# A trunk layer with differential attention on eight cores: first loads packed piece by piece, and an earlier gate for the first V pieces

## The chip, the cores and the metric

The kernel runs on the 8 cores of one Trainium2 chip. Every core runs the same program on its own part of the sequence. The metric is the device time of the slowest core in microseconds, and the time shown is the median of the runs.

## What is computed

The reference is one layer of a decoder trunk on x (4 batches, 4096 positions, 1024 channels, float32). Cut to what matters:

```python
z = h @ w_in                    # (B, S, 3072): q, k, v, attention gate, pool input, pool gate, 512 columns each
o = diff_attention(q, k, v, lam)            # causal, 4 heads, two softmaxes per head, their difference times v
attn_out = rms_norm(o, subln_g) * (1 - lam_init) * silu(g_attn)
pool_out = multiscale_pool(u, w_pool, scale) * silu(g_pool)     # trailing means over 2, 4, 8, 16 positions
h = layer_norm(ALPHA * h + concat(attn_out, pool_out) @ w_out)
h = h + (p @ w_pe) * sigmoid(h @ w_pg + b_pg)
```

## The kernel before

A batch belongs to two cores. Its 4096 positions are four groups of eight blocks of 128 positions; of each group a core owns four blocks and computes their output, and for the other four it computes only K and V, which its own queries need. The projections, the attention, the pooling and the output stage of a core are one long program on TensorE, in which the attention of a group (QK, exp on ScalarE, PV) is woven into the projections of the next one.

**What sets the order.** Every step is a node with a cost, the buffers that it reads and writes, and a key. The planner (class Sched, its run at L264) simulates the engines and the DMA rings: on each engine it takes the node with the smallest key among those that are ready. The instructions are then written out in that order, each with the semaphore waits that its buffers need (Prog.op, Prog.dma, Prog.flush). A gate on a load is a buffer in its list of reads: the issuing engine waits for what last wrote that buffer. Issues of DMAs have the key -10000, so they go first on their engine. All DMA instructions of the trace are put down to L153, the line in flush that issues them, and all matmuls of the kernel's helper mmf to L542.

**The start.** Two weights and two blocks of x are wanted first. They come in five pieces along the contraction index k (eight chunks of 128): PIECES = (0,2), (2,4), (4,6), (6,7), (7,8). A chunk is 128 rows of 512 float32, so a piece of two chunks is 128 rows of 4 KB, a piece of one is 128 rows of 2 KB.

- SP loads the five pieces of the own blocks' x (xT_d[1]) and ACT the five pieces of the K weight (win_d[SEC_K]) as float32 into a staging area that is later mixT. Neither waits for anything.
- For each piece DVE casts x to bf16 (L607) into X[:, 0] and ACT casts K's weight (L609) into its place in W (win).
- POOL loads the five pieces of the V weight (win_d[SEC_V]) straight into W, cast to bf16 on the way. The list GI says for which x piece each V piece waits: GATES[i] is the staging buffer of x piece GI[i], counted from 0.
- Behind them POOL loads the five pieces of the other blocks' x (xT_d[0]) into X[:, 1], then the whole weight sections Q, a block of constants (cst), GA, a halo (xh), U, GP and w_pool. All of these wait for the last x piece (GATE).

TensorE runs twelve matmuls on zeros as a warm-up and then three projections whose loop over the pieces is outermost (function outer, L1151): K of the own blocks (v1, with five warm-up matmuls behind each of the first three pieces), V of the own blocks (v2) and K of the other blocks (v3), 32 matmuls each. Piece i of a projection waits for piece i of the weight and of x. Their keys are fixed numbers counted up in hk, so their order on TensorE is fixed. Behind v3 come V of the other blocks, Q, and the rest by the planner.

In the trace sb_mixT<-xT are SP's x pieces, sb_mixT<-w_in ACT's K pieces, sb_W<-w_in POOL's V pieces and sections, and sb_X<-xT POOL's pieces of the other x, and later whole blocks of x (load_x, L592). The matmuls of v1 and v3 are psum_all<-sb_X,sb_W, those of v2 psum_all<-sb_W,sb_X, and V of the other blocks again psum_all<-sb_W,sb_X.

Before the change the host lays x out as [8 groups of blocks][128 partitions][8 chunks][512] and w_in as [6 sections][128 partitions][8 chunks][512], so the rows of a piece are 16 KB apart.

Of the kernel before, what the change touches and what calls it, by code (L numbers as in the profile page):

```python
# [20 lines left out]
POOL_W = (2, 4, 8, 16)  # L21
OWN = {0: [0, 3, 4, 7], 1: [1, 2, 5, 6]}
VW = 130
GI = (3, 4, 4, 4, 4)
PIECES = [(0, 2), (2, 4), (4, 6), (6, 7), (7, 8)]
SEC_Q, SEC_K, SEC_V, SEC_GA, SEC_U, SEC_GP = range(6)

# [42 lines left out]
class Prog:  # L70
# [48 lines left out]
    def dma(self, Q, out, in_, ds, reads=(), writes=(), turn=False):  # L119
        self._deps(Q, reads, writes)  # L120
        ds.cnt += 16
        t = (ds.sem, ds.cnt)
        _SNAP[(ds.sem.num, ds.cnt)] = dict(Q.seen)
        Q.ops.append(("turn" if turn else "dma", out, in_, ds.sem))
        self._mark(t, reads, writes)
# [327 lines left out]
def build_nc():  # L453
# [3 lines left out]
    xT_d = din("xT", [8, 128, 8, GT])  # L457
# [3 lines left out]
    win_d = din("w_in", [6, 128, 8, 512])  # L461
# [10 lines left out]
    with ExitStack() as top:  # L472
        P = Prog(nc, top)
        PE, ACT, DVE, POOL, SP = P.PE, P.ACT, P.DVE, P.POOL, P.SP

        def sb(name, shape, dt):
            return top.enter_context(nc.sbuf_tensor("sb_" + name, shape, dt))
# [9 lines left out]
        X = sb("X", [128, 2, 8, GT], BF16)  # L487
# [28 lines left out]
        win = W[:].rearrange("p (s k n) -> p s k n", s=6, k=8)  # L516
# [4 lines left out]
        B_x = [[Buf() for _ in PIECES] for _ in range(2)]  # L521
        B_st = [[Buf() for _ in PIECES] for _ in range(2)]
        B_w = [[Buf() for _ in (PIECES if s in (SEC_K, SEC_V) else [0])] for s in range(6)]
# [58 lines left out]
        def dma(Q, out, in_, reads, writes, kb, key=None, ds=None, run=4096):  # L582
            G.add([(Q, 650.0 if Q is POOL else 430.0 if Q is ACT else 400.0, None)], reads, writes, dma=(out, in_, ds or P.dsem(), kb, False, run),
                  key=key, slack=-1e4)
# [11 lines left out]
        def load_sec(s):  # L596
            dma(POOL, win[:, s], win_d[s], GATE, B_w[s], 2048)

        GATE, GATES = [B_st[0][4]], [[B_st[0][k]] for k in GI]
        stage = mixT[:].rearrange("p a n -> p (a n)").bitcast(F32).rearrange("p (s k n) -> p s k n", s=2, k=8)  # L600
        for i, (a, z) in enumerate(PIECES):
            s = slice(a, z)
            dma(SP, stage[:, 0, s, :], xT_d[1][:, s, :], [], [B_st[0][i]], 256 * (z - a))
            dma(ACT, stage[:, 1, s, :], win_d[SEC_K][:, s, :], [], [B_st[1][i]], 256 * (z - a))
        for i, (a, z) in enumerate(PIECES):
            s = slice(a, z)
            G.add([(DVE, 75 + (z - a) * 278.0, [lambda e, s=s: e.tensor_copy(out=X[:, 0, s, :], in_=stage[:, 0, s, :])])],  # L607
# [1 line left out]
            G.add([(ACT, CA((z - a) * 512), [lambda e, s=s: e.activation(out=win[:, SEC_K, s, :], in_=stage[:, 1, s, :], func=AF.Copy)])],  # L609
                  [B_st[1][i]] + B_mix[4 + a // 2], [B_w[SEC_K][i]])  # L610
        for i, (a, z) in enumerate(PIECES):
            dma(POOL, win[:, SEC_V, a:z, :], win_d[SEC_V][:, a:z, :], GATES[i], [B_w[SEC_V][i]], 256 * (z - a))
        for i, (a, z) in enumerate(PIECES):
            dma(POOL, X[:, 1, a:z, :], xT_d[0][:, a:z, :], GATE, [B_x[1][i]], 256 * (z - a))
        load_sec(SEC_Q)
        dma(POOL, cst, cst_d, GATE, [B_cst] + B_U, 546)
        load_sec(SEC_GA)
# [636 lines left out]

_NC_CACHE = {}

def _host_inputs(x, p, w_in, lam_q1, lam_k1, lam_q2, lam_k2, subln_g, w_pool, pool_scale,
                 w_out, ln_g, ln_b, w_pe, w_pg, b_pg):
    f = lambda a: np.ascontiguousarray(np.asarray(a, dtype=np.float32))
    x, p = f(x), f(p)  # L1260
    rows = lambda a, k: np.ascontiguousarray(f(a).reshape(k, 128, -1).transpose(1, 0, 2))
    common = {
        "w_in": np.ascontiguousarray(f(w_in)[0].reshape(8, 128, 6, 512).transpose(2, 1, 0, 3)),
        "w_pool": np.ascontiguousarray(f(w_pool)[0].transpose(1, 0, 2)),
        "w_out": rows(f(w_out)[0], 8), "w_pe": rows(f(w_pe)[0], 2), "w_pg": rows(f(w_pg)[0], 8),
        "ln_g": f(ln_g)[0].reshape(1, 1024), "ln_b": f(ln_b)[0].reshape(1, 1024), "b_pg": f(b_pg)[0].reshape(1, 1024),
    }
    lamv = np.concatenate([f(lam_q1)[0], f(lam_k1)[0], f(lam_q2)[0], f(lam_k2)[0]])
    rep = lambda v: np.broadcast_to(v, (128, v.size))
    pscale = f(pool_scale)[0].reshape(4, 128).T  # L1270
    kk = np.arange(128)[:, None]
    qq = np.arange(128)[None, :]
    tri = (qq >= kk).astype(np.float32)
    in_maps = []
    for c in range(8):
        b, r = c // 2, c % 2
        own, oth = OWN[r], OWN[1 - r]
        xb = x[b].reshape(4, 8, 128, D_MODEL)
        xT = np.empty((8, 128, 8, GT), np.float32)
        for g in range(4):  # L1280
            for k, blks in ((0, oth), (1, own)):
                xT[2 * g + k] = xb[g][blks].reshape(GT, 8, 128).transpose(2, 1, 0)
        x_own = np.ascontiguousarray(xb[:, own].reshape(2048, D_MODEL))
        xh = np.zeros((4, 4, 16, D_MODEL), np.float32)
        for g in range(4):
            for i, o in enumerate(own):
                s = (8 * g + o) * 128
                if s > 0:
                    xh[g, i] = x[b, s - 16:s]
        xh = np.ascontiguousarray(xh.reshape(4, 64, 8, 128).transpose(0, 3, 2, 1))  # L1290
        pT = np.ascontiguousarray(p[0, b].reshape(4, 8, 128, 256)[:, own].reshape(2048, 2, 128).transpose(2, 1, 0))
        masks = np.zeros((128, 2, 2, 128), np.float32)
        for par in range(2):
            masks[:, par, 1, :] = tri
            masks[:, par, 0, :] = 1.0 if (par == 1) == (r == 0) else 0.0
        cnt = np.zeros((128, 4, 16), np.float32)
        t = np.arange(16, dtype=np.float32)
        for pi, w in enumerate(POOL_W):
            cnt[:, pi, :] = 1.0 / np.minimum(t + 1.0, float(w)) if own[0] == 0 else 1.0 / float(w)
        m = dict(common)  # L1300
        cst = np.ascontiguousarray(np.concatenate([rep(f(subln_g)[0]), pscale, cnt.reshape(128, 64), rep(lamv),
                                                   np.eye(128, dtype=np.float32), masks.reshape(128, 512)], axis=1))
        m.update({"xT": xT, "x_own": x_own, "xh": xh, "pT": pT, "cst": cst})
        in_maps.append(m)
    return in_maps
# [13 lines left out]
```

How the kernel before makes its waits and increments, by code:

```python
        def run(S, e):  # L135
            pend = []
            for o in S.ops:
                if o[0] == "wait":
                    pend.append(o)
                elif o[0] == "op":
                    for w in pend[:-1]:
                        e.wait_ge(w[1], w[2])
                    ins = o[1](e)
                    if pend:
                        ins._wait_ge(pend[-1][1], pend[-1][2])
                    pend = []
                    if o[2]:
                        ins.then_inc(S.sem, 1)
                else:
                    for w in pend:
                        e.wait_ge(w[1], w[2])
                    pend = []
                    (e.dma_start_transpose if o[0] == "turn" else e.dma_start)(out=o[1], in_=o[2]).then_inc(o[3], 16)
            for w in pend:
                e.wait_ge(w[1], w[2])
            S.ops = []
```

## Time and profile before

| | us |
|---|---|
| median of 3 runs | 598.72 (598.18 to 599.36) |
| the profiled execution | 599.14 |
| its span on the slowest core, core 3 | 597.6 |
| spans of its eight cores | 592.3 to 597.6 |
| TensorE busy on core 3 | 581.3 (97%) |
| ScalarE, VectorE, GpSimd busy on core 3 | 370.5, 347.8, 81.9 |
| DMA on core 3 | 40311 packets, 48.84 MB, mean 82 GB/s |

Times of rows count from the first instruction of the core's span. Engines are PE (TensorE, with PEld for its weight loads), DVE (VectorE), ACT (ScalarE), POOL (GpSimd) and SP (SyncE). GB/s and the size of a DMA count the bytes written, so a load that casts float32 to bf16 reads twice what is shown. PEclk is the granted clock of TensorE as a share of full speed.

### The profile page before, as it was taken

The page shows a single profiled execution, that of the slowest core. Times are in us where ns is not written, and L with a number is a line of the kernel's source. Part 1 is how long each engine was busy: PE and PEld are TensorE (multiplying, and loading weights), DVE is VectorE, ACT ScalarE, POOL GpSimd, SP SyncE. Part 2 cuts the span into 40 slices and gives each one's busy share as a digit, 9 for nine tenths or more (in the row PEclk, how much of TensorE's full clock was granted, in tenths as well). Part 3 has the DMA queues.
Part 4 walks back from the last instruction along what each step waited for, and adds up shares of the span by engine and source line. Part 5 has one row for each costly group of instructions (what it writes and reads, how often), then busy time and mean ns, then how long its engine had stood idle before and what let it go on. Part 6 is the DMA issues. An engine that isn't in the chain of part 4 may idle for free.

```text
span 597.6 us, 12491 instructions; the slowest of 8 cores (592.3 to 597.6 us)
## 1 busy us (share of the span) xinstructions
PE 581.3 (97%) x5265; PEld 327.3 (55%) x5265; DVE 347.8 (58%) x839; ACT 370.5 (62%) x504; POOL 81.9 (14%) x110
## 2 busy tenths in 40 slices
PE   6889999999999999999999999999999999999996
PEld 2334544454555555666666565676665566565443
DVE  1111892149344386343434578877666787778887
ACT  1213634454654565878788887887887686766342
POOL 0601300040000300000022012021100010010210
PEclk8989999999999999999999999999999999999999
DMA  7799733100340004020654037222413443334442
GB/s 226 128 176 174 135 63 58 36 10 15 70 78 1 9 16 78 6 74 8 126 100 80 2 59 185 36 69 83 129 22 92 100 93 100 82 95 109 110 129 106
DMA packets 40311, 48.84 MB, mean 82 GB/s; under 512 B 30016, under 2 KB 31424, under 8 KB 38592
## 3 DMA queue, kind: packets, MB, share of 16 engines
q0 software_dynamic: 8672, 19.57, 19.8%
q1 hardware_dynamic: 30864, 26.39, 16.0%
q10 hardware_dynamic: 720, 2.10, 1.2%
q8 instruction: 41, 0.67, 0.5%
q14 instruction: 14, 0.11, 0.1%
HBM read 52.73 MB, written 8.39 MB: 102 GB/s over the span
## 4 chain that ended last, share of the span: by engine, by line
PE 87%; DMA 5%; DVE 4%; issue 1%; POOL 1%; ACT 1%; SPq 0%; DVEq 0%; POOLq 0%; ACTq 0%
PE psum_all L542 65%; PE psum_all L830 22%; DMA sb_mixT<-xT 3%; DMA sb_X<-xT 2%; DVE sb_X L570 1%; DVE sb_X L562 1%; DVE sb_W L570 1%; POOL sb_W L153 0%; DVE sb_st L984 0%; ACT sb_W L992 0%; ACT sb_PT L805 0%; POOL sb_mv L1000 0%; DVE sb_gps L570 0%; POOL sb_ms L860 0%; SPq L153 0%
## 5 line engine op out<-in xcount | busy, mean ns | idle before, releaser
L805 ACT ACTIVATE sb_PT<-psum_all 128x1024 bf16<-128x1024 f32 (+1 forms) x276 | 263.7, 1009 | 65.3 <-PE psum_all L542 65.1
L542 PE MATMUL psum_all<-sb_X,sb_W 128*128 128x512 bf16 x640 | 153.8, 384 | 5.7 <-ACT sb_W L609 3.7
L830 PE MATMUL psum_all<-sb_Vt,sb_PT 128*128 128x129 bf16 x2176 | 156.3, 220 | 0.0
L830 PEld LDWEIGHTS psum_all<-sb_Vt,sb_PT 128*128 128x128 bf16 x2176 | 132.2, 98 | 41.7 <-issue 12.8
L542 PEld LDWEIGHTS psum_all<-sb_X,sb_W 128*128 128x128 bf16 x640 | 59.8, 99 | 73.1 <-issue 6.7
L542 PE MATMUL psum_all<-sb_W,sb_X 128*128 128x512 bf16 x384 | 92.2, 380 | 2.0 <-DMA sb_W<-w_in 2.0
L542 PE MATMUL psum_all<-sb_mixT,sb_kT 64*128 64x128 bf16 (+2 forms) x1288 | 83.7, 255 | 0.0
L542 PE MATMUL psum_all<-sb_W 128*128 128x512 bf16 (+1 forms) x328 | 79.7, 374 | 0.5 <-DVE sb_W L580 0.5
L562 DVE TENSOR_TENSOR sb_PT<-sb_PT,sb_masks 128x256 bf16<-128x256 bf16 x128 | 39.8, 319 | 66.9 <-ACT sb_PT L805 65.9
L542 PEld LDWEIGHTS psum_all<-sb_mixT,sb_kT 64*128 64x128 bf16 x1288 | 42.8, 94 | 46.2 <-ACT sb_PT L805 20.3
L542 PE MATMUL psum_all<-sb_W,sb_mixT 128*128 128x512 bf16 x256 | 62.3, 379 | 0.3 <-ACT sb_PT L805 0.3
L542 PEld LDWEIGHTS psum_all<-sb_W,sb_X 128*128 128x128 bf16 x384 | 34.9, 98 | 40.2 <-DMA sb_W<-w_in 3.4
L570 DVE SCALAR_TENSOR_TENSOR sb_X<-sb_X,sb_mv,sb_MI 128x1024 f32<-128x1024 f32 (+1 forms) x33 | 41.2, 1247 | 7.6 <-POOL sb_mv L1000 7.4
L860 POOL TENSOR_TENSOR sb_ms<-sb_ms,sb_mhalf 128x3 f32<-128x3 f32 (+1 forms) x24 | 22.7, 945 | 165.1 <-DVE sb_ms L570 165.0
L542 PEld LDWEIGHTS psum_all<-sb_W 128*128 128x128 bf16 x328 | 29.6, 98 | 27.7 <-issue 1.4
L570 DVE SCALAR_TENSOR_TENSOR sb_gps<-sb_gps,psum_all 128x512 f32<-128x512 f32 (+1 forms) x49 | 32.9, 672 | 16.1 <-ACT sb_gps L552 14.5
L542 PEld LDWEIGHTS psum_all<-sb_W,sb_mixT 128*128 128x128 bf16 x256 | 23.3, 98 | 23.5 <-ACT sb_PT L805 0.5
L552 ACT ACTIVATE sb_gps<-psum_all 128x512 f32<-128x512 f32 (+1 forms) x37 | 21.7, 585 | 21.6 <-PE psum_all L542 21.3
L570 DVE SCALAR_TENSOR_TENSOR sb_X<-sb_X,psum_all 128x512 f32<-128x512 f32 x32 | 21.9, 684 | 18.8 <-PE psum_all L542 18.7
L579 ACT ACTIVATE sb_kT<-psum_all 128x512 bf16<-128x512 f32 x24 | 14.1, 597 | 28.3 <-PE psum_all L542 28.1
L562 DVE TENSOR_TENSOR sb_MI<-sb_MI 128x572 f32<-128x572 f32 (+3 forms) x40 | 29.5, 737 | 0.7
L570 DVE SCALAR_TENSOR_TENSOR sb_mixh<-sb_TA,sb_ms,sb_ga 128x128 bf16<-128x128 f32 x64 | 22.3, 349 | 12.9 <-POOL sb_ms L860 11.9
(98 smaller groups left out, 375.7 us busy)
## 6 DMA issues: line engine op xcount, KB each, us to landing
sb_X<-x_own SPq DMA_DIRECT2D x16, 512.0 KB, 3.7
sb_X<-xT POOLq DMA_DIRECT2D x6, 1024.0 KB, 8.4
out<-sb_X SPq DMA_DIRECT2D x12, 512.0 KB, 3.3
sb_W<-w_in POOLq DMA_DIRECT2D x4, 1024.0 KB, 31.4
sb_W<-w_out POOLq DMA_DIRECT2D x1, 2048.0 KB, 15.3
sb_W<-w_pg POOLq DMA_DIRECT2D x2, 1024.0 KB, 8.6
out<-sb_X SPq DMA_DIRECT2D x7, 256.0 KB, 2.1
sb_mixT<-w_in ACTq DMA_DIRECT2D x3, 512.0 KB, 13.3
```

Of the source, the lines that this page charges most:

```text
L542: return lambda e: e.matmul(out(), lhsT, rhs, start=start, stop=stop, skip_group_check=skip)
L552: G.add([(ACT, CA(n), [lambda e: e.activation(out=out, in_=in_(), func=func, scale=scale)])], reads, writes, slack=slack)
L562: fn = lambda e: e.tensor_tensor(out=out, in0=a() if callable(a) else a, in1=b, op=op)
L570: dve(lambda e: e.scalar_tensor_tensor(out=out, in0=c(a), scalar=s, in1=c(b), op0=op0, op1=op1), reads, writes, n, slack)
L579: G.add([(ACT, CA(n), [lambda e: e.activation(out=out, in_=in_(), func=AF.Copy)]), (DVE, CD(n * x), [lambda e: e.tensor_copy(out=out, in_= ...
L805: G.add([(ACT, CA(2 * w), [lambda e, vb=vb, w=w, pb=pb: e.activation(out=PT[:, pb, :, 0:w], in_=ps[:, vb[0].real:vb[0].real + 2, 0:w], fun ...
L830: return e.matmul(ps[:, 6 + c, col:col + 129], PT[:, pb, c, o:o + 128], Vt[:, kb, h, 0:129], start=st, stop=False, skip_group_check=True)
L860: G.add([(POOL, 350.0 + 210 * np_, [lambda e: e.tensor_tensor(out=ms[:, 1, 0:np_], in0=ms[:, 1, 0:np_], in1=mhalf[:, 0:np_], op=ALU.pow)]) ...
```

## The change

GI goes from (3, 4, 4, 4, 4) to (2, 3, 4, 4, 4): V piece 0 waits for x piece 2, V piece 1 for x piece 3, the others for x piece 4 as before. The host writes the pieces of the K weight, the V weight and of the first two blocks of x (own and other) one behind the other, each piece as [128][its chunks][512], and the loads read them there through the new helper part. The tiles on the chip, the casts and the matmuls stay as they are.

```diff
--- before.py
+++ after.py
@@ -21,7 +21,7 @@
 POOL_W = (2, 4, 8, 16)
 OWN = {0: [0, 3, 4, 7], 1: [1, 2, 5, 6]}
 VW = 130
-GI = (3, 4, 4, 4, 4)
+GI = (2, 3, 4, 4, 4)
 PIECES = [(0, 2), (2, 4), (4, 6), (6, 7), (7, 8)]
 SEC_Q, SEC_K, SEC_V, SEC_GA, SEC_U, SEC_GP = range(6)
 
@@ -596,12 +596,16 @@
         def load_sec(s):
             dma(POOL, win[:, s], win_d[s], GATE, B_w[s], 2048)
 
+        def part(src, a, z):
+
+            return src.rearrange("p k n -> (p k n)")[a * 65536:z * 65536].rearrange("(p k n) -> p k n", p=128, k=z - a)
+
         GATE, GATES = [B_st[0][4]], [[B_st[0][k]] for k in GI]
         stage = mixT[:].rearrange("p a n -> p (a n)").bitcast(F32).rearrange("p (s k n) -> p s k n", s=2, k=8)
         for i, (a, z) in enumerate(PIECES):
             s = slice(a, z)
-            dma(SP, stage[:, 0, s, :], xT_d[1][:, s, :], [], [B_st[0][i]], 256 * (z - a))
-            dma(ACT, stage[:, 1, s, :], win_d[SEC_K][:, s, :], [], [B_st[1][i]], 256 * (z - a))
+            dma(SP, stage[:, 0, s, :], part(xT_d[1], a, z), [], [B_st[0][i]], 256 * (z - a))
+            dma(ACT, stage[:, 1, s, :], part(win_d[SEC_K], a, z), [], [B_st[1][i]], 256 * (z - a))
         for i, (a, z) in enumerate(PIECES):
             s = slice(a, z)
             G.add([(DVE, 75 + (z - a) * 278.0, [lambda e, s=s: e.tensor_copy(out=X[:, 0, s, :], in_=stage[:, 0, s, :])])],
@@ -609,9 +613,9 @@
             G.add([(ACT, CA((z - a) * 512), [lambda e, s=s: e.activation(out=win[:, SEC_K, s, :], in_=stage[:, 1, s, :], func=AF.Copy)])],
                   [B_st[1][i]] + B_mix[4 + a // 2], [B_w[SEC_K][i]])
         for i, (a, z) in enumerate(PIECES):
-            dma(POOL, win[:, SEC_V, a:z, :], win_d[SEC_V][:, a:z, :], GATES[i], [B_w[SEC_V][i]], 256 * (z - a))
+            dma(POOL, win[:, SEC_V, a:z, :], part(win_d[SEC_V], a, z), GATES[i], [B_w[SEC_V][i]], 256 * (z - a))
         for i, (a, z) in enumerate(PIECES):
-            dma(POOL, X[:, 1, a:z, :], xT_d[0][:, a:z, :], GATE, [B_x[1][i]], 256 * (z - a))
+            dma(POOL, X[:, 1, a:z, :], part(xT_d[0], a, z), GATE, [B_x[1][i]], 256 * (z - a))
         load_sec(SEC_Q)
         dma(POOL, cst, cst_d, GATE, [B_cst] + B_U, 546)
         load_sec(SEC_GA)
@@ -1254,6 +1258,10 @@
 
 _NC_CACHE = {}
 
+def _in_pieces(a):
+
+    return np.concatenate([a[:, s:e].ravel() for s, e in PIECES]).reshape(a.shape)
+
 def _host_inputs(x, p, w_in, lam_q1, lam_k1, lam_q2, lam_k2, subln_g, w_pool, pool_scale,
                  w_out, ln_g, ln_b, w_pe, w_pg, b_pg):
     f = lambda a: np.ascontiguousarray(np.asarray(a, dtype=np.float32))
@@ -1265,6 +1273,8 @@
         "w_out": rows(f(w_out)[0], 8), "w_pe": rows(f(w_pe)[0], 2), "w_pg": rows(f(w_pg)[0], 8),
         "ln_g": f(ln_g)[0].reshape(1, 1024), "ln_b": f(ln_b)[0].reshape(1, 1024), "b_pg": f(b_pg)[0].reshape(1, 1024),
     }
+    for k in (SEC_K, SEC_V):
+        common["w_in"][k] = _in_pieces(common["w_in"][k])
     lamv = np.concatenate([f(lam_q1)[0], f(lam_k1)[0], f(lam_q2)[0], f(lam_k2)[0]])
     rep = lambda v: np.broadcast_to(v, (128, v.size))
     pscale = f(pool_scale)[0].reshape(4, 128).T
@@ -1280,6 +1290,8 @@
         for g in range(4):
             for k, blks in ((0, oth), (1, own)):
                 xT[2 * g + k] = xb[g][blks].reshape(GT, 8, 128).transpose(2, 1, 0)
+        for k in range(2):
+            xT[k] = _in_pieces(xT[k])
         x_own = np.ascontiguousarray(xb[:, own].reshape(2048, D_MODEL))
         xh = np.zeros((4, 4, 16, D_MODEL), np.float32)
         for g in range(4):
```

## Rows read from the trace of the kernel before

**Rows 1.** Spans of the cores, with the mean granted clock.

```profile
core 3: 597.6 us, clock 0.993
...
core 5: 597.4 us, clock 0.990
...
core 7: 592.3 us, clock 0.997
```

**Rows 2.** Engines by stretch, core 3: length, busy time (instructions), clock, DMA share, GB/s.

```profile
44.00:144.00 100.00, 100.00 (x637) 49.13 (x636) 50.35 (x130) 45.66 (x81) 17.04 (x20) 1.00 0.42 74
```

**Rows 3.** All waits of PE from 44 us to the end: in total, times, longest.

```profile
PE psum_all L1044 <- DVE sb_W L570: 0.8, 1, 0.8
PE psum_all L542 <- DVE sb_W L580: 0.5, 1, 0.5
PE psum_all L872 <- DVE sb_mv L574: 0.5, 1, 0.5
PE psum_all L542 <- ACT sb_PT L805: 0.3, 1, 0.3
```

**Rows 4.** Chain that ended last, core 3, 0 to 46 us: start, length, what.

```profile
2.44 15.89 DMA sb_mixT<-xT
...
19.68 0.52 issue
20.20 2.09 POOL sb_W L153 x4
22.29 12.14 DMA sb_X<-xT
```

**Rows 5.** Timeline of core 3: start, length, instruction, idle time before it and releaser.

```profile
17.01 0.69 DVE L607 CAST sb_X<-sb_mixT 128x1024 bf16<-128x1024 f32 x1 [2.65 <-DMA sb_mixT<-xT]
...
18.36 0.43 DVE L607 CAST sb_X<-sb_mixT 128x512 bf16<-128x512 f32 x1 [0.66 <-DMA sb_mixT<-xT]
...
19.66 0.43 DVE L607 CAST sb_X<-sb_mixT 128x512 bf16<-128x512 f32 x1 [0.88 <-DMA sb_mixT<-xT]
...
24.50 1.90 PE L542 MATMUL psum_all<-sb_W,sb_X 128*128 128x512 bf16 x8 [1.03 <-DMA sb_W<-w_in]
...
34.88 8.75 PE L542 MATMUL psum_all<-sb_X,sb_W 128*128 128x512 bf16 x32 [2.01 <-DMA sb_X<-xT]
...
43.47 6.85 PE L542 MATMUL psum_all<-sb_W,sb_X 128*128 128x512 bf16 x31
```

**Rows 6.** Timeline of core 7: second K projection and what follows it.

```profile
31.52 7.07 PE L542 MATMUL psum_all<-sb_X,sb_W 128*128 128x512 bf16 x32 [0.30 <-issue]
...
38.42 7.07 PE L542 MATMUL psum_all<-sb_W,sb_X 128*128 128x512 bf16 x32
```

**Rows 7.** Stretches of the start on core 3, columns as in rows 2.

```profile
2.40:8.00 5.60, 5.21 (x12) 1.55 (x12) 0.00 (x0) 1.28 (x1) 0.00 (x0) 1.00 0.89 208
8.00:13.00 5.00, 2.21 (x8) 0.97 (x9) 0.69 (x1) 1.06 (x1) 0.00 (x0) 0.87 0.99 302
2.40:18.30 15.90, 12.19 (x36) 4.22 (x37) 2.08 (x3) 4.44 (x4) 0.00 (x0) 0.89 0.88 261
18.30:19.70 1.40, 1.40 (x8) 0.64 (x7) 0.46 (x2) 0.64 (x2) 0.70 (x1) 1.00 0.06 22
19.70:21.00 1.30, 1.30 (x8) 0.59 (x7) 0.39 (x1) 0.63 (x1) 0.80 (x2) 1.00 0.18 5
21.00:34.40 13.40, 9.90 (x44) 3.80 (x42) 2.58 (x4) 2.17 (x4) 7.66 (x15) 1.00 1.00 124
34.40:39.50 5.10, 4.62 (x14) 1.83 (x15) 0.00 (x0) 0.00 (x0) 0.00 (x0) 0.67 1.12 193
```

**Rows 8.** DMA of core 3 from 44 to 66 us.

```profile
DMA packets 809, 3.93 MB, mean 179 GB/s; under 512 B 91, under 2 KB 335, under 8 KB 391
```

**Rows 9.** DMA of core 3 from 569 to 573 us, GB/s in 40 slices of 0.1 us.

```profile
GB/s 0 0 0 0 0 0 0 0 0 0 0 164 164 164 0 0 0 0 246 164 369 246 614 287 369 614 246 451 532 246 369 0 0 0 0 0 0 0 0 0
DMA packets 144, 0.52 MB, mean 131 GB/s; under 512 B 16, under 2 KB 16, under 8 KB 144
```

## The prediction

> **What bounds the kernel now.** I read the cores first. The time is that of the slowest core, core 3, with core 5 next and core 7 the fastest, 5.3 us less than core 3 [rows 1]. The question is where core 3 loses these 5.3 us, and the answer lies before 44 us. From 44 to 144 us its TensorE is busy for all of 100.00 us [rows 2], and from 44 us to the end the waits that TensorE has on other engines are four, 0.8, 0.5, 0.5 and 0.3 us, 2.1 us together [rows 3]. So whatever time the start gives up or wins is carried to the end nearly one for one. The two cores show it: the next work behind the second K projection begins at 43.47 us on core 3 and at 38.42 us on core 7 [rows 5, 6], 5.05 us apart, and the spans differ by 5.3.
>
> The start is bound by transfers. The chain of core 3 [rows 4] reads: 15.89 us until the fourth x piece has landed, behind it (not shown) POOL's issue of the first V piece, a pause of 0.52 us until POOL has the fifth piece, 2.09 us for the four other V issues, and 12.14 us from the issue of the other block's first x piece to its landing, which lets TensorE go on. The timeline of the same stretch [rows 5] shows TensorE's side of it: it stands still for 1.03 us before the first V piece and for 2.01 us before the second K projection, which waits for x. That projection then takes 8.75 us for 32 matmuls, 7.07 on core 7 [rows 6]: the granted clock of 34.4 to 39.5 us was 0.67 [rows 7], a mean of the two levels 1.2 and 2.4 GHz, right behind the waiting. The stretches of the DMA [rows 7] show two kinds of limit. From 2.4 to 18.3 us and from 21.0 to 34.4 us the engines are busy, shares 0.88 and 1.00: there their rate counts. Between the two, from 18.3 to 21.0 us, they move almost nothing (shares 0.06 and 0.18): the first loads are done and the V pieces, which POOL may issue only once x pieces four and five are in, have not begun.
>
> **The change part by part.** *The gate.* V piece one now waits for x piece three instead of four, V piece two for four instead of five, the other three for five as before. On core 3 these pieces are in, by the start of their casts [rows 5], at 17.01, 18.36 and 19.66 us. So the first V issue moves by 18.36 - 17.01 = 1.35 us, the second by 19.66 - 18.36 = 1.30. Nothing stands in POOL's queue ahead of them, and behind the fifth gate there are three V issues in place of four; at 2.09 / 4 = 0.52 us each [rows 4], the x issues and the weight sections behind them come 0.52 us earlier. What that does to the landing of x has two ends. If only its own issue counted, it would be 0.52 us. If the engines are what it waits for, it is the whole 1.35 us, because the V bytes then begin earlier in a stretch where the engines had nothing to do. The share of 1.00 from 21.0 us on speaks for the second, and I take 1.35. Do the earlier V bytes get in the way of the last x and K pieces? V data begins to move some 2.5 us behind its gate (gate at 18.36, a rate of 5 GB/s in 19.7 to 21.0 and full load only after, rows 5 and 7). From a gate at 17.01 that is about 19.5 us, and the first loads have only 22 GB/s left from 18.3 to 19.7. On core 3 the two hardly meet: nothing. On a core whose pieces come further apart they would meet, but what the last K pieces lose there the V pieces have won, and the second K projection waits for both.
>
> *The layout.* The same bytes go in transfers of the same number and size, from the same queues; on the chip's side a row of a piece stays one run of 4 KB (2 KB for the two small pieces), and rows now follow each other without the 16 KB step. No row shows this for these loads, so I bound it. The chain holds 15.89 + 12.14 = 28.0 us of transfer. The rate now is 261 GB/s in the first loads and, because the V and x pieces are cast on the way and the page counts the written half, 2 x 124 = 248 GB/s read in 21.0 to 34.4 us [rows 7]. The lower end is a stretch of the same rows: from 2.4 to 8.0 us the first loads ran at 208 GB/s. The upper end are the whole weight sections, which lie in one piece in memory with rows of 16 KB: 179 GB/s written from 44 to 66 us, that is up to 358 read [rows 8]. The nearest row by far is an x_own load, 128 rows of 4 KB that follow each other in memory, just what the pieces become: 0.52 MB between 570.1 and 572.1 us [rows 9], 260 GB/s, though alone on the engines. That is the rate of today. I stay close to it and take a tenth of the way to the upper end, (358 - 261) / 10, some 10 GB/s or 4%: 28.0 x (1 - 261 / 271) = 1.03 us.
>
> Here a rule speaks against the layout as a gain. The Trainium skill, DMA: Bandwidth & Descriptors, section "Latency and other measured facts", has copies at a row pitch of 512 KiB near full rate (207 of 214 GB/s) and a clear loss only from a pitch of 2 MiB up. By that rule a pitch of 16 KB costs nothing, the second term is zero and the sum is 1.35 us; the x_own row agrees, with 260 beside 261 GB/s.
>
> *The order.* The planner puts the gates into its own clock, so it may write another order. Up to the second K projection TensorE's order hangs on fixed keys. Behind it the V, x and weight transfers all move together. What a new order could win is at most the 2.1 us of waits left [rows 3]; what it could lose I bound by as much again, and I take zero, since the same work meets the same transfers a little earlier.
>
> *The sum.* 1.35 + 1.03 = 2.4 us off the profiled execution, which took 599.14 us (its span of 597.6 and 1.5 around it): 596.7. The median of the runs shown is 598.72, 0.42 below the profiled one, so the same step gives 596.3. All of that holds if core 3 stays typical of the slowest core; core 5, 0.2 us behind it, has the same gates.
>
> **The rivals.** *The layout does nothing.* Each row was one run before and is one run after, and the x_own row stands at today's rate. Then only the gate counts: 598.72 - 1.35 = 597.4, and with the smaller end of the gate, 0.52, 598.2. For it speaks rows 9, against it that x_own was alone on its engines while the first loads come on two queues. The rule on the row pitch named above would give the same time. Chance 0.30.
>
> *The layout does a lot.* If rows that follow each other can be read at the sections' 358 GB/s, the chain loses 28.0 x (1 - 261 / 358) = 7.6 us, and 1.35 with it: 589.8. Half of that rate gain would give about 593.6. For it speaks that the sections do reach this rate on the same core a few us later; against it that their rows are four times as long. TensorE could follow: in the stretch from 2.4 to 34.4 us it has waits to give up, and the slow clock of core 3, 8.75 - 7.07 = 1.7 us, could go too. Chance 0.14.
>
> *The packed pieces read worse.* Sixteen engines and two queues then work in two stretches of 512 KB at a time, where each piece was spread over 2 MB. Its place is the first loads, its price the slowest stretch, 208 GB/s, held throughout: 15.89 x (261 / 208 - 1) = 4.05 us, less 1.35 from the gate: 2.7 us slower, 601.4. It decides from 15.89 x (261 / r - 1) = 1.35, r = 241 GB/s, downwards. For it speaks that the early stretch was slow at all with the engines 0.89 busy; against it the 302 GB/s just behind it in the same layout [rows 7] and the x_own row. Chance 0.14.
>
> **How the numbers follow.** The forecast has what is left, 0.42, and its own range is 595.5 to 597.2: a fifth of the way to the upper rate in place of a tenth, 28.0 x (1 - 261 / 280) = 1.9 us, or the smaller gate, 0.52 us. About 0.2%, 1.2 us, is what a measurement of this kernel can tell from no change; that line lies at 597.5, beside the rival in which the layout does nothing. Faster: 0.36 of the forecast, nearly half of that rival (0.12) and all of the large gain (0.14), together 0.62. Slower: most of the last rival, 0.11, and 0.01 from a worse order, 0.12. The rest, 0.26, is within. The range runs from 592.2, which leaves out the far half of the large gain, to 600.2, which leaves out most of the slow case.
>
> **What would show it.** Right: POOL's first V issue about 0.6 us behind the third x piece; no empty stretch between the first loads and the V pieces; x of the other block landing near 32 us instead of 34.4 on the slowest core; rates of 265 to 280 GB/s in the first loads; waits of TensorE from 44 us on as before. Wrong: a rate in the first loads of 300 or more (the large gain) or under 241 (the slow case); x landing only 0.5 us earlier with the gap closed (the engines were not what it waited for); or new waits of TensorE behind 44 us, which would be the order.

## The result and the profile after

The changed kernel takes 593.24 us (median of 4 runs, 592.39 to 594.58) beside 598.66 us of the kernel before: a ratio of 0.9911, 95% interval 0.9889 to 0.9932, or 5.3 us less. The forecast was 596.3, 2.4 us less than the median shown, with a range down to 592.2. So the sign and the range held, and the gain is more than twice the one forecast. The times below are medians of all executions of a kernel, a few of which were slow; the ratios and their intervals leave those out and compare with the kernel before on the same chip.

All cores have won: the mean of their eight spans went from 595.3 to 590.3 us. In this execution they also lie closer together. Before they ran from 592.3 to 597.6 us [rows 1]; after, they run from 589.0 to 591.4, with four cores within 0.2 us at the top:

```profile
core 1: 591.2 us, clock 1.000
...
core 3: 591.3 us, clock 0.997
core 4: 591.4 us, clock 0.997
...
core 7: 591.4 us, clock 0.997
```

That is not a property of the changed kernel: in a second profile of it (e8 below) the spans run from 589.0 to 595.3 us.

The start of the slowest core, now core 4, in the same stretches as rows 7 (length, busy time with the count of instructions for PE, PEld, DVE, ACT and POOL, then PEclk, DMA share, GB/s written):

```profile
2.40:8.00 5.60, 5.22 (x12) 1.56 (x12) 0.00 (x0) 1.28 (x1) 0.00 (x0) 1.00 0.94 226
8.00:13.00 5.00, 2.42 (x9) 1.02 (x10) 1.39 (x2) 2.02 (x2) 0.00 (x0) 0.86 0.93 297
2.40:18.30 15.90, 12.94 (x40) 4.76 (x41) 2.51 (x4) 4.98 (x5) 0.88 (x2) 0.89 0.90 264
18.30:19.70 1.40, 1.40 (x8) 0.68 (x7) 0.43 (x1) 0.73 (x2) 0.66 (x2) 1.00 0.83 94
19.70:21.00 1.30, 1.25 (x7) 0.59 (x7) 0.00 (x0) 0.00 (x0) 1.30 (x4) 1.00 1.08 129
21.00:34.40 13.40, 12.54 (x59) 5.44 (x59) 2.58 (x4) 2.17 (x4) 6.34 (x12) 1.00 1.09 152
```

Two things are to be seen beside rows 7. The empty stretch from 18.3 to 21.0 us has filled, from DMA shares of 0.06 and 0.18 to 0.83 and 1.08. And the first loads run as before (264 against 261 GB/s), while V and the other x have gone from 124 to 152 GB/s written. The second was not forecast at that size.

The timeline of core 4 (start, length, instruction, idle time before it and its releaser), to be laid beside rows 5:

```profile
15.64 0.69 DVE L611 CAST sb_X<-sb_mixT 128x1024 bf16<-128x1024 f32 x1 [3.26 <-DMA sb_mixT<-xT]
...
16.25 0.70 POOL L153 DMA_DIRECT2D sb_W<-w_in  x1 [15.55 <-DMA sb_mixT<-xT]
...
17.58 0.43 DVE L611 CAST sb_X<-sb_mixT 128x512 bf16<-128x512 f32 x1 [1.25 <-DMA sb_mixT<-xT]
...
18.12 0.54 POOL L153 DMA_DIRECT2D sb_W<-w_in  x1 [1.17 <-DMA sb_mixT<-xT]
18.89 0.43 DVE L611 CAST sb_X<-sb_mixT 128x512 bf16<-128x512 f32 x1 [0.89 <-DMA sb_mixT<-xT]
...
19.40 1.59 POOL L153 DMA_DIRECT2D sb_W<-w_in  x3 [0.74 <-DMA sb_mixT<-xT]
...
22.41 7.07 PE L542 MATMUL psum_all<-sb_W,sb_X 128*128 128x512 bf16 x32
...
30.29 7.07 PE L542 MATMUL psum_all<-sb_X,sb_W 128*128 128x512 bf16 x31 [0.81 <-DVE sb_Vt L580]
...
37.19 7.07 PE L542 MATMUL psum_all<-sb_W,sb_X 128*128 128x512 bf16 x31
```

The gates are there as the change says: a V issue 0.6 us behind the third x piece, one behind the fourth, three behind the fifth. On this core TensorE now does the whole V projection in one go of 32 matmuls, where core 3 had waited three times, 1.03, 0.47 and 0.47 us (of the other seven cores only core 0 does so too, the rest wait once, 0.40 to 1.41 us, for a V piece); before the second K projection it waits 0.81 us, not 2.01; and that projection takes 7.07 us, not 8.75. The profile puts the end of the 0.81 us down to VectorE's eviction of V (L580), but it was the other block's x again: the last share of its first piece landed at 29.83 us, and the projection begins 0.46 us behind that, as it does on core 3 before (34.42 and 34.88 us) and on core 7 after (29.43 and 29.89 us), where the profile names x. What follows starts at 37.19 us, and from there to the end of the span are 591.4 - 37.19 = 554.2 us; on core 3 before it was 597.6 - 43.47 = 554.1. The waits of TensorE from 44 us on, which answer to rows 3 (in total, times, longest):

```profile
PE psum_all L542 <- issue: 1.6, 10, 0.2
PE psum_all L1048 <- DVE sb_W L570: 0.8, 1, 0.8
PE psum_all L542 <- DVE sb_W L580: 0.5, 1, 0.5
PE psum_all L876 <- DVE sb_mv L574: 0.5, 1, 0.5
PE psum_all L542 <- ACT sb_PT L809: 0.3, 1, 0.3
...
```

The four of rows 3 stand there unchanged (lines below L600 have moved by four). The first row is ten gaps of 0.2 us at most; this trace has 5179 matmuls for 5265 weight loads, so these look like records that are missing, not waits. On these two cores the whole difference is made before that point and is carried to the end one for one. As far as the traces name them, each engine's steps stand in the same order before and after: the planner's clock moves as a whole, and its list does not change. The forecast's worry about a new order falls away.

### The profile page after: what moved, and what is told of

Its sections match the earlier page's. It is cut to its first block, busy times and chain, and to the rows that moved or that the text cites. A ratio compares the mean times of both kernels' runs of the same rounds, so it can differ in the third digit from the quotient of the medians.

```text
span 591.4 us, 12406 instructions; the slowest of 8 cores (589.0 to 591.4 us)
## 1 busy us (share of the span) xinstructions
PE 573.3 (97%) x5179; PEld 327.1 (55%) x5265; DVE 348.0 (59%) x839; ACT 370.5 (63%) x504; POOL 82.0 (14%) x110
## 4 chain that ended last, share of the span: by engine, by line
PE 84%; DVE 8%; issue 2%; ACT 2%; DMA 1%; POOL 1%; DVEq 0%; ACTq 0%
PE psum_all L542 64%; PE psum_all L834 21%; DVE sb_X L570 2%; DMA sb_mixT<-w_in 1%; DVE sb_X L562 1%; DVE sb_W L570 1%; POOL sb_ms L864 1%; DVE sb_st L988 1%; ACT sb_PT L809 1%; DVE sb_gps L570 1%; DVE sb_MI L562 0%; DVE sb_TA L570 0%; ACT sb_W L996 0%; POOL sb_mv L1004 0%; DVE sb_mixh L570 0%
## 5 line engine op out<-in xcount | busy, mean ns | idle before, releaser
L542 PE MATMUL psum_all<-sb_X,sb_W 128*128 128x512 bf16 x613 | 147.0, 381 | 5.4 <-ACT sb_W L613 3.0
L542 PE MATMUL psum_all<-sb_W,sb_X 128*128 128x512 bf16 x366 | 88.4, 379 | 1.5 <-issue 0.6
L542 PE MATMUL psum_all<-sb_W 128*128 128x512 bf16 (+1 forms) x308 | 75.7, 374 | 2.0 <-issue 0.6
L542 PE MATMUL psum_all<-sb_W,sb_mixT 128*128 128x512 bf16 x240 | 59.0, 379 | 1.3 <-ACT sb_PT L809 0.3
L570 DVE SCALAR_TENSOR_TENSOR sb_X<-sb_X,sb_mv,sb_MI 128x1024 f32<-128x1024 f32 (+1 forms) x33 | 41.2, 1249 | 7.6 <-POOL sb_mv L1004 7.4
L542 PEld LDWEIGHTS psum_all<-sb_W 128*128 128x128 bf16 x328 | 29.6, 98 | 27.6 <-issue 1.4
L570 DVE SCALAR_TENSOR_TENSOR sb_gps<-sb_gps,psum_all 128x512 f32<-128x512 f32 (+1 forms) x49 | 33.0, 673 | 16.0 <-ACT sb_gps L552 14.5
L570 DVE SCALAR_TENSOR_TENSOR sb_X<-sb_X,psum_all 128x512 f32<-128x512 f32 x32 | 21.9, 684 | 17.6 <-PE psum_all L542 17.5
L570 DVE SCALAR_TENSOR_TENSOR sb_mixh<-sb_TA,sb_ms,sb_ga 128x128 bf16<-128x128 f32 x64 | 22.4, 349 | 14.1 <-POOL sb_ms L864 13.1
## 6 DMA issues: line engine op xcount, KB each, us to landing
sb_W<-w_in POOLq DMA_DIRECT2D x4, 1024.0 KB, 27.6
```

The source lines that it names most:

```text
L542: return lambda e: e.matmul(out(), lhsT, rhs, start=start, stop=stop, skip_group_check=skip)
L570: dve(lambda e: e.scalar_tensor_tensor(out=out, in0=c(a), scalar=s, in1=c(b), op0=op0, op1=op1), reads, writes, n, slack)
```

## The experiments

Three theories stood: the gate and the layout each give a part, the gate gives all, the layout gives all. Besides the times I read three figures from the traces, averaged over the eight cores. In the traces each of these transfers raises its semaphore in sixteen steps, as its sixteen shares land; "last share" is when the other block's first x piece is complete, and "lag" the time between its first and its last share. The rate is GB/s written from 21.0 to 34.4 us. These three figures come from one execution of each kernel, on several chips; the row of e8, the changed kernel once more, shows how far they repeat.

| kernel | ratio to before, 95% interval | rate | last share, us | lag, us |
|---|---|---|---|---|
| before | 1 | 135 | 32.8 | 3.7 |
| changed | 0.9911 (0.9889 to 0.9932) | 156 | 28.4 | 2.1 |
| e8, the changed kernel again | 0.9923 (0.9907 to 0.9939) | 152 | 29.3 | 2.3 |
| e1, packed, old gates | 0.9942 (0.9926 to 0.9958) | 146 | 30.3 | 1.9 |
| e2, new gates, old layout | 0.9980 (0.9969 to 0.9992) | 129 | 31.9 | 4.2 |
| e3, new gates, first loads packed | 0.9968 (0.9955 to 0.9980) | 135 | 31.2 | 4.0 |
| e4, new gates, V and other x packed | 0.9942 (0.9929 to 0.9956) | 150 | 29.3 | 1.8 |
| e12, new gates, rows 16 KB apart in own tensors | 0.9970 (0.9957 to 0.9983) | 135 | 31.5 | 4.6 |
| e9, the same, 18 KB | 0.9908 (0.9887 to 0.9929) | 158 | 28.3 | 1.6 |
| e5, the same, 20 KB | 0.9915 (0.9901 to 0.9929) | 153 | 29.0 | 1.5 |
| e10, the same, 24 KB | 0.9942 (0.9917 to 0.9966) | 147 | 29.7 | 2.4 |
| e11, the same, 32 KB | 0.9943 (0.9923 to 0.9963) | 147 | 29.7 | 2.0 |

**e1, the layout alone.**

```diff
-GI = (2, 3, 4, 4, 4)
+GI = (3, 4, 4, 4, 4)
```

> The packed layout with the gates as before (V piece 0 behind x piece 3, the others behind x piece 4). The changed kernel took 593.2 us, the kernel before 598.7. Theory 'both': by the landings of the two traces, averaged over the eight cores, the fourth x piece is in 1.5 us earlier and the stretch from the first V issue to the landing of the other block's first x piece is 1.1 us shorter, which is the layout's; the rest is the gate's. Then 598.7 - 2.6 = 596.1. Theory 'gate alone' (the rates rose for another reason, the layout does nothing): 598.7. Theory 'layout alone': 593.2.

Measured: 596.08 us, ratio 0.9942, by the ratio 3.5 us less than the kernel before. That rules out "gate alone" (a ratio of 1), and the interval leaves out "layout alone" (0.991). It is more than the 2.6 us that "both" had for the layout. That 596.08 stands on the 596.1 of "both" is chance: on this chip the kernel before took 599.67 us, not 598.7.

**e2, the gates alone.**

```diff
-            dma(SP, stage[:, 0, s, :], part(xT_d[1], a, z), [], [B_st[0][i]], 256 * (z - a))
+            dma(SP, stage[:, 0, s, :], xT_d[1][:, s, :], [], [B_st[0][i]], 256 * (z - a))
...
-    for k in (SEC_K, SEC_V):
+    for k in ():
```

(the same for the three other loads, and no packing of x on the host)

> The old layout with the new gates. Theory 'both': the gate is worth the 1.8 us between the third and the fourth x piece, averaged over the cores of the changed kernel (1.35 by the prediction): 598.7 - 1.8 = 596.9. Theory 'gate alone': 593.2. Theory 'layout alone': 598.7.

Measured: 598.45 us, ratio 0.9980, by the ratio 1.2 us (0.5 to 1.9) less than the kernel before. "Layout alone" falls with it; the gate's own share is near the 1.35 us of the prediction, though the interval reaches down to its smaller end, 0.52. Its slowest core shows what the gate leaves. TensorE's timeline on core 1:

```profile
21.95 1.89 PE L542 MATMUL psum_all<-sb_W,sb_X 128*128 128x512 bf16 x8
25.11 1.90 PE L542 MATMUL psum_all<-sb_W,sb_X 128*128 128x512 bf16 x8 [1.27 <-DMA sb_W<-w_in]
27.45 3.63 PE L542 MATMUL psum_all<-sb_W,sb_X 128*128 128x512 bf16 x16 [0.44 <-DMA sb_W<-w_in]
33.36 8.75 PE L542 MATMUL psum_all<-sb_X,sb_W 128*128 128x512 bf16 x32 [2.28 <-DMA sb_X<-xT]
```

V begins right behind K, since its first piece is in time. But the later pieces come more slowly than TensorE takes them: it waits for the second and the third, and then 2.28 us for the other x; behind that wait the projection takes 8.75 us as on core 3 before. From 33.36 to 42.00 us the granted clock was 0.80 in the mean. It was at the lower level, 1.2 GHz, in one stretch and at 2.4 GHz in the rest (columns as in rows 7):

```profile
34.44:37.85 3.41, 3.41 (x10) 1.21 (x9) 0.00 (x0) 0.00 (x0) 0.00 (x0) 0.50 1.12 193
```

**e3 and e4, half of the layout each.** e3 packs x's own block and the K weight only, e4 V and the other x only; both have the new gates.

```diff
-            dma(POOL, win[:, SEC_V, a:z, :], part(win_d[SEC_V], a, z), GATES[i], [B_w[SEC_V][i]], 256 * (z - a))
+            dma(POOL, win[:, SEC_V, a:z, :], win_d[SEC_V][:, a:z, :], GATES[i], [B_w[SEC_V][i]], 256 * (z - a))
```

(e3, which also leaves the other x's load and both host arrays as before; e4 does the same with the two loads of SP and ACT instead)

> The new gates, with only the first loads (own x and the K weight, on SP and ACT) packed; V and the other x, on POOL, as before. Theory 'both': it lacks the 1.1 us of the shorter V and x stretch: 593.2 + 1.1 = 594.3. If the layout counts in the first loads alone (two queues at once): 593.2. If it counts on POOL's queue alone: as the gate alone, 596.9.

Measured: 597.30 us, ratio 0.9968, by the ratios 0.7 us less than with the gates alone, which the intervals don't tell from nothing.

> The new gates, with only V and the other x packed; own x and the K weight as before. Theory 'both': it lacks the 1.5 us of the earlier fourth x piece: 593.2 + 1.5 = 594.7. If the layout counts in the first loads alone: 596.9. If it counts on POOL's queue alone: 593.2.

Measured: 595.89 us, ratio 0.9942, by the ratios 2.3 us less than with the gates alone. Against the values of "both", 594.3 and 594.7 or as ratios 0.9927 and 0.9933, e3 is far off and e4 within its interval (0.9929 to 0.9956). Most of the layout's gain is on POOL's queue: packing V and x alone gives 2.3 us, packing the first loads alone 0.7. Taking the same packing away from the changed kernel costs more, 3.4 and 1.9 us (2.7 and 1.1 by e8), so the part of the first loads lies somewhere from 0.7 to 1.9 us. The lag goes with POOL's queue too, 4.2 us with nothing packed and 4.0 with the first loads packed, but 1.8 us with V and x packed. The first share of the piece comes at the same time in e2 and e4, 27.8 and 27.6 us; it is the last one that comes 2.6 us earlier. So in this pair the layout does not make every share quicker, it keeps some of them from falling behind.

**e5, e9 to e12: packing, or the step between rows?** A packed piece has rows 4 KB apart in place of 16. These runs keep the old order of bytes and only change the step: K, V and two blocks of x are copied by the host into tensors of their own, with unused chunks behind the eight. No piece is contiguous in any of them.

```diff
+    wkv_d = din("w_kv", [2, 128, 10, 512])
+    x01_d = din("x_01", [2, 128, 10, 512])
...
+            dma(POOL, X[:, 1, a:z, :], x01_d[0][:, a:z, :], GATE, [B_x[1][i]], 256 * (z - a))
...
+def _wide(a):
+    out = np.zeros((2, 128, 10, 512), np.float32)
+    out[:, :, :8] = a
```

(10 chunks are 20 KB; 8, 9, 12 and 16 the others)

> The new gates and the old order of the bytes, but with the rows of K, V and both blocks of x 20 KB apart in memory instead of 16 KB (a host-made copy with two unused chunks behind the eight); no piece is contiguous. With the old layout and the new gates the first and the last sixteenth of the other block's first x piece landed 4.2 us apart on a mean core, with the packed one 2.1 us. Theory 'step': rows 16 KB apart make some of the sixteen shares lag, and another step frees them: spread near 2 us, time near the changed kernel's ratio, 0.991 of the kernel before. Theory 'packing': only rows that follow each other help: spread near 4 us, ratio 0.998 as with the gate alone. Theory 'shares differ by themselves' (noise of the day): anything between, and the spread does not go with the time.

Measured: 594.23 us, ratio 0.9915, and a lag of 1.5 us: as good as packed, without packing. TensorE's timeline on its slowest core, core 4, has none of the long waits of e2:

```profile
21.99 1.90 PE L544 MATMUL psum_all<-sb_W,sb_X 128*128 128x512 bf16 x8
24.46 5.42 PE L544 MATMUL psum_all<-sb_W,sb_X 128*128 128x512 bf16 x24 [0.57 <-DMA sb_W<-w_kv]
30.13 7.07 PE L544 MATMUL psum_all<-sb_X,sb_W 128*128 128x512 bf16 x31 [0.26 <-issue]
37.04 7.07 PE L544 MATMUL psum_all<-sb_W,sb_X 128*128 128x512 bf16 x31
```

"Packing" as the cause falls: rows that do not follow each other do as well. But the copies also lie elsewhere in memory, so the other steps and a control had to follow.

> As the run with rows 20 KB apart, with rows 18 KB apart (one unused chunk of 2 KB behind the eight). Theory 'step': any step that is no large power of two frees the lagging shares: spread of the other block's first x piece near 2 us, ratio near 0.9915. Rival '4 KB of padding is needed': spread between 2 and 4 us, ratio 0.993 to 0.997.

Measured: 593.02 us, ratio 0.9908, lag 1.6 us. Two KB of padding are enough.

> Rows 24 KB apart (three times 8 KB). Theory 'step': what counts is the power of two in the step; 24 KB has 8 KB where 20 KB has 4 KB and 16 KB has 16 KB: spread near 2 us or a little over, ratio 0.991 to 0.994. Rival 'only odd multiples of 4 KB help': spread near 4 us, ratio 0.998.

Measured: 595.28 us, ratio 0.9942, lag 2.4 us, in between, though the interval of the ratio overlaps with that of 20 KB and with that of 16 KB in own tensors. In the first loads the steps stand in another order: the second and third x piece lag 3.2 and 2.9 us here, 1.7 and 1.8 at 20 KB, but 2.2 and 1.6 at 16 KB (e12).

> Rows 32 KB apart, twice the old step. Theory 'step': the lagging shares lag at least as much as with 16 KB: spread 4 us or more, ratio 0.998 or above, up to 1.002. Rival 'the step of 16 KB alone is bad' (or the copies in tensors of their own are what helps): spread near 2 us, ratio 0.9915.

Measured: 594.99 us, ratio 0.9943, lag 2.0 us. Here the theory "step" as I had written it is wrong: twice the step is not worse than the old one. Rate and lag are better, and the ratio lies clear of that of e2; with that of e12 its interval just overlaps.

> The control for the runs with other steps: the same copies of K, V and two blocks of x in tensors of their own, with rows 16 KB apart, as in the kernel before; new gates. So far: in the old tensors, 16 KB apart, ratio 0.998 and 4.2 us between the first and the last sixteenth of the other block's first x piece; in tensors of their own, 18 and 20 KB apart, 0.991 and 0.992 with 1.6 and 1.5 us; 24 and 32 KB apart, 0.994 both, with 2.4 and 2.0 us. Theory 'step': the rows 16 KB apart are what makes shares lag, ratio 0.998, about 4 us. Rival 'place': the old tensors' place in memory was bad, and moving the bytes helps whatever the step: ratio 0.994 or less, near 2 us, and then the step is worth only what lies between 0.994 and 0.991.

Measured: 597.51 us, ratio 0.9970, lag 4.6 us. The control comes back to the gates alone (0.9980): the place in memory is worth nothing that these runs can tell, and for V and the other x the step is what counts. The stretch from 21.0 to 34.4 us of the control and of the run with 20 KB, on the same four cores (columns as above):

```profile
core 4: us, PE busy (x) PEld busy (x) DVE busy (x) ACT busy (x) POOL busy (x), PEclk, DMA share, GB/s
21.00:34.40 13.40, 9.88 (x44) 3.90 (x43) 2.57 (x4) 2.17 (x4) 6.77 (x13) 1.00 0.99 131
core 5: us, PE busy (x) PEld busy (x) DVE busy (x) ACT busy (x) POOL busy (x), PEclk, DMA share, GB/s
21.00:34.40 13.40, 11.14 (x46) 4.51 (x44) 2.57 (x4) 2.17 (x4) 6.33 (x13) 0.87 1.01 129
core 6: us, PE busy (x) PEld busy (x) DVE busy (x) ACT busy (x) POOL busy (x), PEclk, DMA share, GB/s
21.00:34.40 13.40, 10.32 (x47) 4.22 (x46) 2.58 (x4) 2.17 (x4) 6.20 (x12) 1.00 1.02 133
core 7: us, PE busy (x) PEld busy (x) DVE busy (x) ACT busy (x) POOL busy (x), PEclk, DMA share, GB/s
21.00:34.40 13.40, 9.64 (x39) 3.73 (x38) 2.38 (x4) 1.97 (x4) 6.05 (x12) 0.93 1.04 136
```

That was 16 KB; the run with 20 KB:

```profile
core 4: us, PE busy (x) PEld busy (x) DVE busy (x) ACT busy (x) POOL busy (x), PEclk, DMA share, GB/s
21.00:34.40 13.40, 12.53 (x56) 5.13 (x56) 2.58 (x4) 2.17 (x4) 6.67 (x13) 1.00 1.08 149
core 5: us, PE busy (x) PEld busy (x) DVE busy (x) ACT busy (x) POOL busy (x), PEclk, DMA share, GB/s
21.00:34.40 13.40, 12.04 (x55) 5.00 (x54) 2.56 (x4) 2.16 (x4) 5.52 (x11) 1.00 1.08 158
core 6: us, PE busy (x) PEld busy (x) DVE busy (x) ACT busy (x) POOL busy (x), PEclk, DMA share, GB/s
21.00:34.40 13.40, 12.93 (x60) 5.37 (x58) 2.58 (x4) 2.17 (x4) 6.16 (x12) 1.00 1.08 155
core 7: us, PE busy (x) PEld busy (x) DVE busy (x) ACT busy (x) POOL busy (x), PEclk, DMA share, GB/s
21.00:34.40 13.40, 12.75 (x59) 5.33 (x57) 2.58 (x4) 2.17 (x4) 5.67 (x11) 1.00 1.06 156
```

What changes is not the DMA share: it is near 1 or above in both. A share says that packets are under way, not that they come quickly. The rate differs, 129 to 136 against 149 to 158 GB/s on these four cores and 129 to 144 against 142 to 158 on all eight, and in this stretch, on all eight, TensorE gets 39 to 47 matmuls done in one case and 55 to 60 in the other.

**e6 to e8: can the gates go further?** e6 moves every V gate one x piece earlier again, e7 also drops the third group of warm-up matmuls, e8 is the changed kernel beside them on the same chip.

```diff
-GI = (2, 3, 4, 4, 4)
+GI = (1, 2, 3, 4, 4)
...
-                if warm and i < 3:
+                if warm and i < 2:
```

(the second edit in e7 only)

> The changed kernel with every V gate one x piece earlier still: V pieces 0, 1 and 2 wait for x pieces 1, 2 and 3 (GI = 1, 2, 3, 4, 4). Theory 'TensorE binds now': on the changed kernel's slowest core V follows K without a wait, and what is left is 0.8 us before the second K projection; at most 0.8 us faster than the changed kernel, ratio 0.990. Rival 'the V bytes now meet the last x and K pieces': the first loads end later, the K projection with them, up to 1 us slower than the changed kernel, ratio 0.993.

> The gates of the run before this one and no warm-up matmuls behind the third x piece (two groups of five instead of three). In the changed kernel these five stand between the third and the fourth piece on TensorE, 1.08 us, while both are there. Theory 'TensorE binds from the third piece on': a further 1.0 us, ratio 0.9885. Rival 'V or x binds again': no more than the run before. Rival 'the clock falls without them': the K' or V projection takes 8.7 instead of 7.07 us on some cores, ratio 0.993 or more.

> The changed kernel itself once more, beside the others on their chip: ratio 0.991.

Measured: 593.58 us and 0.9899 (0.9886 to 0.9912) for e6, 593.69 us and 0.9897 (0.9884 to 0.9910) for e7, 595.41 us and 0.9923 (0.9907 to 0.9939) for e8. So the changed kernel came out at 0.9911 and 0.9923 in two sets of runs, and e6 is 1.4 us faster than it on the same chip, a little more than the 0.8 that I had allowed, with intervals that just overlap. Its ratio and that of e7 are the lowest of this study, but 0.9911 for the changed kernel and 0.9908 for e9 can't be told from them. In e7 the 1.0 us did not come. TensorE's timeline on its slowest core, core 2, shows why:

```profile
16.18 2.54 PE L542 MATMUL psum_all<-sb_X,sb_W 128*128 128x512 bf16 x11
21.32 1.02 PE L542 MATMUL psum_all<-sb_X,sb_W 128*128 128x512 bf16 x4 [2.60 <-ACT sb_W L613]
22.18 7.07 PE L542 MATMUL psum_all<-sb_W,sb_X 128*128 128x512 bf16 x32
29.08 7.07 PE L542 MATMUL psum_all<-sb_X,sb_W 128*128 128x512 bf16 x31
```

Without the warm-up matmuls TensorE waits 2.60 us for the last K piece instead (0.20 to 1.19 us on six other cores, not at all on core 1). The last pieces are late, and what is new beside them are the V bytes: the fifth x piece landed at 18.5 us in e8, 19.2 in e6 and 19.3 in e7, averaged over the cores, while the fourth came at 17.0 to 17.1 us in all three. The rival that I had named for e6 is there as a mechanism and eats part of the gain. The rival with the falling clock is not there: no core of e7 has a second K projection that takes longer than 7.07 us but for its waits. Behind the last K piece, V and the second K projection run without a break on core 2.

## Why the prediction was right, and where it was off

*What bounds.* Right for this pair. The start decides, transfers bind it, and what is won there reaches the end one for one: 554.1 us behind the second K projection's end on core 3 before, 554.2 on core 4 after. It does not always reach the end. In e8, the same kernel, the slowest core is core 1 with 558.2 us behind that point: at 371 us TensorE waits 2.19 us there for VectorE (L570), and from 372.9 to 376.3 us its clock is at 1.2 GHz. The forecast had looked at core 3 alone from 44 us on [rows 3], where that wait does not occur.

*The gate.* Right in sign, and in size as far as the runs tell: 1.35 us were forecast, 1.2 (0.5 to 1.9) were measured with the gates alone. The empty stretch closed: the mean DMA share of the cores from 18.3 to 21.0 us went from 0.45 before (0.12 on core 3) to 0.83 in e2. The reason for taking 1.35 and not 0.52 us, that x waits for the engines, is borne out only in part. In e2 x comes 32.76 - 31.94 = 0.82 us earlier on the mean core, but its first loads, whose layout and issue are those of before, were also done 0.29 us earlier in that execution (fifth x piece at 18.88 against 19.17 us). What is left, 0.53 us, is x's own issue, which the prediction had named as the sign that the engines are not what x waits for. With everything packed it is otherwise: from e1 to the changed kernel x comes 1.9 us earlier, of which 0.7 are the first loads' own (18.5 and 17.9 us), and to e8, where these end together with those of e1, 1.0 us. So the larger part of the shift seems to reach x only where the loads are packed; with one execution of each kernel that is not more than likely. The first V bytes did not disturb the first loads in the changed kernel; one piece earlier they do, as e6 and e7 show.

*The layout.* The sign was right, the size was off by more than three times, and the reason behind it was wrong. The term was 1.03 us: the 28.0 us of the chain at a rate 4% higher. The layout alone gave 3.5 us (2.5 to 4.4). Three choices in that step failed. I spread the gain evenly over the first loads and POOL's loads; the runs put 0.7 to 1.9 us on the former (whose rate stayed, 264 GB/s against 261 on the slowest cores) and 2.3 to 3.4 on the latter. I took as nearest row an x_own load [rows 9], packed rows 4 KB apart, whose 260 GB/s looked like the rate of today; but that is a mean over a hole. Of its 2.0 us nothing moves from 570.4 to 570.8, and from 570.8 to 572.1 us the DMA view of before shows the rest of the load at a rate near the upper end of 358:

```profile
DMA packets 120, 0.48 MB, mean 366 GB/s; under 512 B 4, under 2 KB 4, under 8 KB 120
```

And that was one transfer alone, while the cost of the old layout showed where many stand in a queue, as a lag between the shares of one transfer. Last, I looked for the cost in the rate alone, when the last share of sixteen is what TensorE waits for. The mean rate in the stretch of V and x rose from 135 to 156 GB/s, and to 146 with the old gates in e1, where V begins later and fills less of it; the lag fell from 3.7 to 2.1 us, in e1 to 1.9.

*The rule on the row pitch.* The Trainium skill, DMA: Bandwidth & Descriptors, section "Latency and other measured facts", finds no loss to speak of at a pitch of 512 KiB and a clear one from 2 MiB up, so the layout's term would have been zero. These runs differ, and they decide: with pieces of 4 KB cut out of rows 16 KB apart the kernel is 0.55% slower than with 20 KB (0.9970 against 0.9915), in the same kind of tensor. What the page says of the remedy agrees: 4 KiB of padding per row brought the rate back at its pitch of 4 MiB, and here 4 KB did, and 2 KB too. With 8 and 16 KB of padding, steps of 24 and 32 KB, the ratios lie in between (0.9942 and 0.9943).

*The rivals.* "The layout does nothing" and "the packed pieces read worse" fell with e1. "The layout does a lot" had the right sense, with a chance of 0.14: its half-way case, 593.6, lies beside the measured 593.2. That nearness is luck: its cause, rows that follow each other being read faster in the whole chain, is not what the runs show, since rows 20 KB apart do as well and the rate of the first loads stayed. (593.6 is also half of the time won and not, as it says, half of the rate gain; by the same sum (261 + 358) / 2 = 309.5 GB/s would give 593.0.) It had named the slow clock of core 3 too, 1.7 us: no core of the changed kernel has a second K projection of that length, the longest is 7.09 us. That part went together with the wait before the projection.

*The range.* The forecast's own range, 595.5 to 597.2, missed. The measured time lies in the whole range because its lower end, 592.2, had been drawn down for the rival in which the layout does a lot.

## What to carry to other kernels

A DMA share of 1.00 says that the engines have work, not that they get through it: where a consumer waits for a whole transfer, look at how far its sixteen shares land apart, in more than one execution, and compare the same bytes at another distance between rows before asking for fewer bytes. Pieces cut out of wide rows on the host's side can be packed, or the rows padded by a chunk; here both left the number of instructions and transfers on the chip as it was. Opening the gate on the later loads 1.35 us earlier was worth 1.2 us here (0.5 to 1.9), and one step further showed as a late last piece of the first loads.

## What the hardware showed that I had not expected

- The distance between the rows of a load mattered at 16 KB for the loads on POOL's queue: lags of 4.2 and 4.6 us and 129 and 135 GB/s written in two different places of memory, against 1.5 and 1.6 us and 153 and 158 GB/s at 20 and 18 KB.
- It is not simply "the larger the power of two, the worse". At 32 KB the lag was 2.0 us and at 24 KB 2.4, with ratios of 0.9943 and 0.9942, between the two. Why 16 KB is the worst of the five there stays open, as does which of the sixteen shares fall behind: the traces do not name them. And it holds for POOL's loads alone. In the first loads, on two other queues and without a cast, the third x piece lagged 3.4 us before but 1.6 in e2 and in e12, all at 16 KB, and 2.9 and 3.0 us at 24 and 32 KB. There the lag differs as much between executions of one layout as between layouts.
- A wait and TensorE's clock can be one cost in two rows. Of the cores that waited some 2 us for the other x, several then had their clock at 1.2 GHz for part of the second K projection and took 8.75 instead of 7.07 us for it (core 3 before, 2.01 us of waiting, lower level from 35.63 to 39.05 us; core 1 of e2, 2.28 us of waiting, 34.44 to 37.85). There a wait of 2 us cost 3.7 in all. It does not always come so: core 2 before waited 2.46 us and core 3 of e2 2.25, and both took 7.07 at 2.4 GHz throughout. With 0.81 us of waiting, on core 4 after, it took 7.07.
